# A chunked delta rule in 64 by 64 quarters of TensorE, with the order of all engines rewritten

## What is computed

```python
a_mat = eye + where(strict, einsum('id,jd->ij', k*beta, k) * decay, 0)
sol   = triangular_solve(a_mat, concat([v*beta, k*beta*exp(gc)]))     # u, w
attn  = where(tri, einsum('id,jd->ij', q, k) * decay, 0)
def step(state, ...):
    v_new = u - w @ state
    o     = q_dec @ state + attn @ v_new
    state = state * exp(glast) + k_dec.T @ v_new
```

## Time and profile before

| | us |
|---|---|
| median of 3 runs | 2786.05 |
| lowest, highest | 2779.52, 2786.98 |
| span of the profiled execution | 2786.4 |
| TensorE busy in it | 2702.5 (97%) |
| VectorE busy | 2107.3 (76%) |
| ScalarE busy | 1287.9 (46%) |
| GpSimd busy | 343.9 (12%) |
| delta rule, first copy of `v_new` to the last chunk's | 212.9 |

### The profile page before, as it was taken

One profiled execution on the slowest core, in us unless ns is written; L12 is line 12 of the kernel. 1 busy time (PEld: TensorE's weight loads), 2 busy tenths in 40 slices (PEclk: granted clock), 3 DMA queues, 4 the chain that ended last, 5 costly groups with the idle time before them and its releaser, 6 DMA issues. The chain is left out here.

```text
span 2786.4 us, 44753 instructions
## 1 busy us (share of the span) xinstructions
PE 2702.5 (97%) x17355; PEld 2277.9 (82%) x17355; DVE 2107.3 (76%) x3262; ACT 1287.9 (46%) x2296; POOL 343.9 (12%) x273
## 2 busy tenths in 40 slices
PE   9999988989999999999999999899999999999998
PEld 7888877888888888888878887788877888888886
DVE  6644445775799999898889885366658999998978
ACT  5323345853454444443356754566543544444332
POOL 0000056340000000000000001365511000000001
PEclk9999999999999999999999999999999999999999
DMA  5323252534322222284322433532042122224652
GB/s 184 121 106 116 81 178 94 151 99 161 119 79 91 83 91 76 107 327 144 107 102 106 152 93 124 175 124 93 18 167 108 63 84 81 91 78 177 238 189 90
DMA packets 162444, 339.08 MB, mean 122 GB/s; under 512 B 35584, under 2 KB 69568, under 8 KB 151616
## 3 DMA queue, kind: packets, MB, share of 16 engines
q1 hardware_dynamic: 143664, 321.54, 32.6%
q10 hardware_dynamic: 18576, 14.75, 1.7%
HBM read 252.17 MB, written 84.05 MB: 121 GB/s over the span
## 5 line engine op out<-in xcount | busy, mean ns | idle before, releaser
L2494 POOL TENSOR_TENSOR ffn_down_rstd<-ffn_down_rstd,ffn_down_power 128x1 f32<-128x1 f32 x15 | 15.0, 1000 | 1263.2 <-DVE ffn_down_rstd L2430 1263.2
L1051 DVE TENSOR_TENSOR even_in_w_lo<-even_in_raw_left,even_in_w_hi 128x512 fp32r<-128x512 f32 x80 | 49.9, 686 | 88.2 <-ACT even_in_w_hi L976 88.2
L934 PE MATMUL even_in_acc<-even_in_w_hi,even_x_hi 128*128 128x512 f32 x256 | 99.6, 389 | 0.0
L935 PE MATMUL even_in_acc<-even_in_w_lo,even_x_hi 128*128 128x512 f32 x256 | 99.6, 389 | 0.0
L936 PE MATMUL even_in_acc<-even_in_w_hi,even_x_lo 128*128 128x512 f32 x256 | 99.6, 389 | 0.0
L4024 DVE SCALAR_TENSOR_TENSOR even_mixed<-even_mixed,odd_qkv_taps 128x1023 f32<-128x1023 f32 (+2 forms) x72 | 92.1, 1281 | 4.9 <-ACT even_mixed L3857 3.2
L3508 DVE CUSTOM_DVE_ANT_0 dil_probs<-dil_bank,dil_mask 128x128 f32<-128x128 f32 (+1 forms) x192 | 56.0, 347 | 38.9 <-PE dil_bank L3417 32.2
L936 PE MATMUL even_in_acc<-even_in_w_hi,even_in_s_lo 128*128 128x512 f32 x192 | 74.7, 389 | 0.0
L934 PE MATMUL even_in_acc<-even_in_w_hi,even_in_s_hi 128*128 128x512 f32 x192 | 74.7, 389 | 0.0
L935 PE MATMUL even_in_acc<-even_in_w_lo,even_in_s_hi 128*128 128x512 f32 x192 | 74.7, 389 | 0.0
L3464 ACT ACTIVATE dil_probs<-dil_probs,dil_neg_peak 128x128 f32<-128x128 f32 (+1 forms) x192 | 70.7, 442 | 2.6 <-DVE dil_neg_peak L3513 2.6
(11 more groups left out here) (881 smaller groups left out, 9221.1 us busy)
## 6 DMA issues: line engine op xcount, KB each, us to landing
ffn_w_raw<-in_ffn_up SPq DMA_DIRECT2D x42, 1024.0 KB, 4.8
even_mixed<-in_ffn_down SPq DMA_DIRECT2D x28, 512.0 KB, 4.1
odd_mixed<-in_ffn_down SPq DMA_DIRECT2D x28, 512.0 KB, 4.0
hp<-even_in_stage SPq DMA_DIRECT2D x13, 1024.0 KB, 4.2
hidden<-even_mixed SPq DMA_DIRECT2D x22, 512.0 KB, 2.6
ffn_w_raw<-in_od_w_qkv SPq DMA_DIRECT2D x11, 1024.0 KB, 5.7
hidden<-odd_mixed SPq DMA_DIRECT2D x22, 512.0 KB, 2.6
even_in_raw_left<-in_ev_w_in SPq DMA_DIRECT2D x10, 1024.0 KB, 5.0
```

The costliest lines, as they stand in the source:

```text
L934: pe.matmul(to, hi[:, tok], wh, start=(opens and k == 0), stop=False, skip_group_check=not opens)
L935: pe.matmul(to, hi[:, tok], wl, start=False, stop=False, skip_group_check=not opens)
L1051: dve.tensor_tensor(w_lo[:, p % 2, k], source(i)[:, k], f32(w_hi[:, p % 2, k]), ALU.subtract).then_inc(lo_ready, 1)
```

## The change

Every 128 by 128 product of the delta rule but the transposes is written as four 64 by 64 quarters with 128 moving columns: `own` are the two whose rows and output columns lie in the same half, `across` the other two. An `across` of a product waits on a semaphore for its `own` (both add into the same bank). In the list, `own` of one product alternates with `across` of another that lies in another bank. `xt` and `attn` have a quarter of zeros, which is left out (`across_lower`). `kk` moves from `c_ps` to `d4_ps`, and `key_values` from `d4_ps` to `c_ps`.

```diff
+            def own(to, q, i, left, right, opens=False, closes=False):
+                h = q * HG + i
+                for half in (low, high):
+                    mm = pe.matmul(to[q][half, i], left[half, h, half], right[half, h], start=opens and i == 0, stop=closes,
+                                   skip_group_check=True)
+                return mm
...
+            def across(to, q, i, left, right, closes=True):
+                h = q * HG + i
+                for half, rows in halves_across:
+                    mm = pe.matmul(to[q][half, i], left[rows, h, half], right[rows, h], start=False, stop=closes,
+                                   skip_group_check=True)
+                return mm
...
+            def wait_qk_own(m, q):
+                if m < 2:
+                    pe.wait_ge(b_done, 2 * m + q + 1)
+                else:
                     pe.wait_ge(y_copied, 2 * (m - 2) + q + 1)
...
+            def keys_0_beside_values_0(n, part):
+                more, prior = n + 1 < TT, n > 0
+                if part == 0 and more:
+                    wait_kk_own(n + 1, 0)
+                if part == 0 and prior:
+                    pe.wait_ge(kv_half, 2 * (n - 1) + 1)
                 pe.sem_inc(tiles_seen, 1)
+                for i in part_heads(part):
+                    if more:
+                        mm = kk_own(n + 1, 0, i)
+                        if i == HG - 1:
+                            mm.then_inc(kk_half, 1)
+                    if prior:
+                        mm = key_values_across(n - 1, 0, i)
+                        if i == HG - 1:
+                            mm.then_inc(kv_done, 1)
```

Thirteen such steps of four heads make up a chunk. The loop's levels 1, 2, 5 and the end of the chunk:

```diff
+                products_x(n, 1, 0)
+                keys_0_beside_values_0(n, 0)
+                products_x(n, 1, 1)
+                keys_0_beside_values_0(n, 1)
+
+                products_b(n, 2, 0)
+                values_1_beside_keys_0(n, 0)
+                products_b(n, 2, 1)
+                values_1_beside_keys_0(n, 1)
+                products_x(n, 2, 0)
+                keys_1_beside_values_1(n, 0)
+                products_x(n, 2, 1)
+                keys_1_beside_values_1(n, 1)
...
+                products_b(n, 5, 0)
+                products_b(n, 5, 1)
+                if prior:
+                    attn_0_beside_q_state_1(n - 1, 0)
+                products_x(n, 5, 0)
+                products_x(n, 5, 1)
+                if prior:
+                    attn_0_beside_q_state_1(n - 1, 1)
+
                 for q in range(2):
+                    last_b_beside_first_x(n, q)
+                if prior:
+                    for part in range(2):
+                        attn_1_beside_0(n - 1, part)
+                for q in range(2):
+                    last_x_beside(n, q)
+                if n > 1:
+                    turn_out(n - 2)
+                for part in range(2):
+                    queries_0_beside_values_0(n, part)
+                for part in range(2):
+                    values_1_beside_queries_0(n, part)
+                for part in range(2):
+                    queries_1_beside_values_1(n, part)
                 if more:
                     for q in range(2):
                         products_b(n + 1, 1, q)
+                    for part in range(2):
+                        values_0_beside_queries_1(n, part)
```

After the loop the last chunk's `outputs` follow in five steps, and then `turn_out(TT - 2)`. The outputs are turned two chunks late instead of one, from `gate`, which `gate_outputs` now overwrites in place of the tile `gated`. So the gate's buffer is free later:

```diff
             def load_gate(m):
                 if m > 1:
-                    sp.wait_ge(gated_done, m - 1)
+                    sp.wait_ge(y_turned, m - 1)
```

The state is faded by one GpSimd operation:

```diff
+            def fade_state(n):
+                pool.wait_ge(state_done, 2 + 2 * n)
+                pool.tensor_tensor(state_d[:], state[:, n % 2], per_head(exp_all[:, n]), ALU.mult).then_inc(state_d_done, 1)
```

More of the change, by code:

```diff
@@ new lines, in part_heads, with keys_of, queries_of, kk_own @@
+            def part_heads(part):
+                return range(2 * part, 2 * part + 2)
+            def keys_of(m):
+                return x_t[:, m % 2, H:2 * H]
+            def queries_of(m):
+                return x_t[:, m % 2, 0:H]
+            def kk_own(m, q, i):
+                return own(d4_ps, q, i, keys_of(m), keys_of(m), opens=True)
+            def kk_across(m, q, i):
+                return across(d4_ps, q, i, keys_of(m), keys_of(m))
+            def qk_own(m, q, i):
+                return own(d4_ps, q, i, keys_of(m), queries_of(m), opens=True)
@@ new lines, in q_state_own, with q_state_across, attn_own, attn_across @@
+            def q_state_own(n, q, i):
+                return own(d4_ps, q, i, q_et[:, n % 2], state[:, n % 2], opens=True)
+            def q_state_across(n, q, i):
+                return across(d4_ps, q, i, q_et[:, n % 2], state[:, n % 2], closes=False)
+            def attn_own(n, q, i):
+                return own(d4_ps, q, i, attn[:, n % 2], v_new[:], closes=True)
+            def attn_across(n, q, i):
+                return across_lower(d4_ps, q, i, attn[:, n % 2], v_new[:])
+            def values_own(n, q, i):
+                return own(v_ps, q, i, xt[:], u[:], opens=True, closes=True)
@@ new lines, in keys_1_beside_values_1 @@
+            def keys_1_beside_values_1(n, part):
+                more, prior = n + 1 < TT, n > 0
+                if part == 0 and more:
+                    wait_kk_own(n + 1, 1)
+                if part == 0 and prior:
+                    pe.wait_ge(kv_half, 2 * (n - 1) + 2)
+                pe.sem_inc(tiles_seen, 1)
+                for i in part_heads(part):
+                    if more:
+                        mm = kk_own(n + 1, 1, i)
+                        if i == HG - 1:
+                            mm.then_inc(kk_half, 1)
+                    if prior:
+                        mm = key_values_across(n - 1, 1, i)
+                        if i == HG - 1:
+                            mm.then_inc(kv_done, 1)
@@ L4685, in products_b, with turn_out @@
+            def turn_out(n):
+                pe.wait_ge(y_done, H * (n + 1))
+                pe.wait_ge(u_done, 2 * min(n + 2, TT - 1) + 2)
+                if n + 2 == TT:
+                    pe.wait_ge(out_copied, n)
+                for h in range(H):
+                    mm = pe.transpose(c_both[:, h], gate[:, n % 2, h], ident[:])
+                mm.then_inc(y_turned, 1)
             def products_b(n, l, q):
```

589 lines of the change are left out of this document (391 added, 198 removed).

## The result

The changed kernel takes 2849.54 us, median of 4 runs (2844.52 to 2854.07), against 2784.35 for the kernel before in the same runs: a ratio of 1.0239, 95% interval 1.0225 to 1.0253. It is 2.4% slower. The forecast was 2795 in a range of 2768 to 2812: the sign was right, the size is seven times too small, and the time lies outside the range.

What follows compares the result with a forecast made beforehand. TensorE was taken to bound the kernel. Seven intervals of 210.5 us against 212.9 give -2.4; with +4.0 at the start and +7.5 at the end, +9.1: 2795 us, range 2768 to 2812.

Steps and rivals of the forecast that it cites:

- c: Rival on TensorE steps: a quarter with 128 moving columns takes only 58 ns, steps 0.46 us; 2786, no change; chance 0.05.
- d: Rival on TensorE steps: quarters of different products do not run beside each other, 1.79 us a step; about 2875; chance 0.03.
- undisturbed chunk: Chunk that waits for no late load: 26.2 us plus 0.9 for code loads, 27.1 against 30.4 before.
- the sum: Per chunk: TensorE work 24.3 us plus added waits 1.9 make 26.2, also taken for the last interval.
- Start: First chunk: qk waits for b_mat, then 56 transposes; first_x 5.2 us later, chunk itself 1.2 shorter, +4.0 us.
- End: After the last chunk: split_hi now stands behind copy_y and copy_out; 14.4 us to the next block, +7.5.
- The load: x_t issued behind the transposes in four chunks: TensorE waits 3.7 us (1.2 to 5.5), plus 2.5 lost to the clock.
- To this come code loads ... I add 0.9: TensorE's stops inside bursts while its code loads: 0.9 us a chunk, with 1.4 times as many records.
- 22.8 us for the transfers: Transfers' part of the seven intervals: four chunks at 32.8 us each where an undisturbed one is 27.1.
- (b): Rival: x_t lands at its worst, long half-clock stretches, code loads behind 3 MB of transfers; 36.3 a chunk, 2810; chance 0.15.
- (a): Rival: load less late, 1.2 us, no clock drop; four chunks of 28.0, 2776, or 2772 if hidden; chance 0.3.

Runs made afterwards that it cites:

- e15: Changed kernel without the unused TensorE increments and with x_t, kv and gate loads of one head from the third chunk on: 2790.21 us.
- e5: Changed kernel with x_t, kv and gate loads cut to one head from the third chunk on, all increments kept: 2826.46 us.
- e2: Changed kernel with three bursts of unused products (quarters with 64 and 128 moving columns, whole) behind the last turn_out: code blocks 3.47 us apart in the first burst.
- e16: Changed kernel with three bursts of unused products behind the last turn_out, an unused increment every 16 records in the first two: 31 increments add 3.2 and 2.75 us.
- e8: Kernel before the change with x_t, kv and gate loads cut to one head from the third chunk on: 2775.93 us.
- e1: Changed kernel with SP issuing the x_t and kv loads ahead of the gate load in each round: 2839.85 us.
- e12: Kernel before the change without TensorE's increments of the semaphore that nothing waits for: 2774.15 us, ratio 0.9964.

## Why the prediction was wrong

**Right.** Quarters with 128 moving columns take 28 ns a record, four beside each other, and the step costs what whole products cost (rivals c and d fall). The work of an undisturbed chunk is 27 to 28 us (e15 less its stops). That the last interval less its stops of 4.6 us is 26.2, the number of the sum, is luck: it has 860 records, 108 fewer than a full one, and the sum did not take them off (before, 26.8 against 30.1). Start: `first_x` 16.55 us into the stage against 11.13, +5.4 for a forecast +5.2; to the first new values 46.9 against 43.7, +3.2 for +4.0, but by one execution of each: others whose start is the same have 44.0 to 44.7 (e5, e2, e16) and 40.1 (e8). End: 14.97 us against 6.97, +8.0 for +7.5, with TensorE waiting for ScalarE's and VectorE's split as described. The load: `x_t` issued behind the transposes, landing 9.3 us after its issue in the median, TensorE waiting 4.2 to 6.0 us where 3.7 and at most 5.5 were forecast, the clock at half for 3.4 to 10.2 us in these chunks. The wait is seen in three of the four; in the first of them a stop of 5.0 us for code stands in its place, and `x_t` is not waited for. They take 41.3 us on average, 5.3 above the second interval; the sum had 5.7 (32.8 less 27.1). That the totals agree is in part luck: the parts were larger than forecast, 5.3 us for each wait and 4.2 a chunk lost to the clock, and a part of them is no loss, for e1 takes the waits away and shortens the intervals by only 9.1 us in all.

**The step that failed** is "To this come code loads ... I add 0.9". Against the forecast the seven intervals miss 59 us: 11.4 and 8.9 in the first two, 8.5 on average in the next four, 4.6 in the last. The stops for code alone are 54.2 us, 7.7 an interval (9.6, 8.5 and 4.6 in the first two and the last, where there is no other stop), for a term of 0.9. I had read the six stops of the earlier trace rows as accidents of transfers and scaled them with the number of records. ("Under 1 us each" was a misreading besides: the rows show 1.41 and 1.45; about 1 us is their mean over the steady chunks, and one of the six is a wait for VectorE.) The rest were the visible end of a rate: a block of some 124 records follows the one before in 3.5 us at best, and in these kernels in 3.7 or more. Before, a chunk of 664 records, 5.3 blocks, took 30 us and the rate was never met except behind a transfer; now 968 records, 7.8 blocks, were to run in 27. 7.8 blocks of 4.0 us are 31 us, more than the work, before any transfer. The arrivals of the blocks were in the trace of before, and 124 records at 15 to 28 ns are 1.9 to 3.5 us: that division was not made. (The 1.4 for the number of records was nearly right: 1.46.)

**The second miss** is a cost that the sum does not have: the 25 increments that the change adds to each chunk. Beside whole products they cost nothing in an undisturbed chunk; at the quarters' pace each costs 0.09 to 0.13 us, most of it as further stops for code, so the 54.2 us above contain it. The two can be told apart by steps. Without its 22.8 us for the transfers the forecast had 187.7 us for the seven intervals. With small loads and no increments (e15) they take 212.8: +25.1, or 3.6 us a chunk on top of the 0.9; 21.7 us of stops for code are in it. All increments kept (e5): 248.6, +35.8. With the full transfers (the changed kernel): 269.7, +21.1 by the late load and the code that it delays, near the forecast's 22.8. In the other order, leaving out all increments gives 31.6 us back and small loads on top of it 25.3 more.

**The rivals.** (b) had the words, "code loads behind 3 MB of transfers", and 2810; it takes the stops only as a matter of transfers, and e5 refutes that as the whole: with them cut to one head the kernel still takes 2826. (a) is refuted by the 16.0 us of waits. That the range did not reach 2849 comes from the same term: I bounded it by the stops seen in a kernel that used code more slowly.

**The rest.** The part of the kernel ahead of the change ended 6.5 us earlier in this execution (1764.97 against 1771.47); +3.2, +56.8, +8.0 and -6.5 make 61.5 of the 61.8. That part is the same code in both. It ran 13.7 us at half clock in this execution and 27.3 in the other, and half of the difference is 6.8: the 6.5 is no effect of the change. In the other runs here, with the same code ahead, the stage begins between 1762.2 and 1771.1.

## What to carry to other kernels

Count instructions per microsecond, not only products: ahead of splitting a product into smaller ones, divide a block of code (some 124 to 128 float32 records here) by the pace of the burst that will run it, and hold it against the distance that the blocks keep. And with small pieces an instruction that was free beside large products, here the increment, comes onto the path; taking out those that nobody needs was worth more here than anything else tried. A load that is moved out of the way of its user may land in the way of the code.

## What the runs showed of the hardware

- TensorE's code came in blocks of 16 KB, 256 instructions; all 32 stops for code in the changed kernel's window ended 1.2 to 1.6 us after a block had landed.
- Code blocks of 128 records followed each other in 3.47 us without any other transfer; in the changed kernel restarts one block apart were 3.75 us or more apart, 4.3 in the median, and without increments and with small loads (e15) 3.9 to 4.3; with 64 moving columns a burst of quarters runs at 26 ns a record on average (12.84 us for 496), not at the 15 of its pace, with 128 at 30, whole products at 112.
- An unused increment on TensorE costs 0.15 us in a row, 0.09 to 0.10 every 16 quarter records, and nothing that can be measured in an undisturbed chunk of whole products (29.97 against 30.06 us, e12).
- With quarters and 3 MB of loads a chunk, the code itself came late by 3.7 to 5.1 us in five of six chunks (e1); with the loads cut to one head no stop was longer than 2.7.
